# A two-block transformer kernel: in the second block the norm's scale moves from the activations to the finished tiles, its shift into ScalarE's functions, and the pooling from GpSimd to VectorE

## What is computed

```
h = rms_norm(x, ln1_g[l]) * (1.0 + sc1) + sh1
z = h @ w_in[l]
u_pool, c_q_raw, c_kv_raw, k_rope_raw, gz_a, gz_b = jnp.split(z, cuts, axis=-1)
y_a = pool_mixer(u_pool, w_pool[l], pool_scale[l]) @ p_pool[l]
y_b = mla(c_q_raw, c_kv_raw, k_rope_raw, ...) @ p_attn[l]
merged = jax.nn.sigmoid(gz_a) * y_a + jax.nn.sigmoid(gz_b) * y_b
x = x + g1 * (merged @ w_out[l])
h2 = rms_norm(x, ln2_g[l]) * (1.0 + sc2) + sh2
x = x + g2 * (jnp.square(jax.nn.relu(h2 @ w_ff1[l])) @ w_ff2[l])
```

## Time and profile before

| | us |
|---|---|
| time, median of 3 runs | 1953.87 (1952.1 to 1955.76) |
| the profiled execution's own time | 1956.42 |
| its span in the trace | 1955.1 |
| TensorE busy with matmuls | 1899.5 (97%) |
| VectorE / ScalarE / GpSimd busy | 1374.3 / 1032.3 / 35.3 |
| second block, from the first leading pair | from about 1243 to the end |

### The profile page before, as it was taken

The page is one execution under the profiler, slowest core; times in us unless marked ns, Lnnn a source line. Parts: engine busy times, 40 slices in busy tenths (PEclk is TensorE's granted clock), DMA queues, the critical chain, the costliest instruction groups (busy, mean ns, idle before and its releaser), DMA issues.

```text
span 1955.1 us, 36640 instructions
## 1 busy us (share of the span) xinstructions
PE 1899.5 (97%) x15339; PEld 1839.7 (94%) x15339; DVE 1374.3 (70%) x2295; ACT 1032.3 (53%) x1728; POOL 35.3 (2%) x56
## 2 busy tenths in 40 slices
PE   7999999999999999999999999899999998999998
PEld 6999988899999999989889999889999998999998
DVE  5777666577776677666568777677897566788854
ACT  5444555565444544455666444566554456655433
POOL 0000000000000000000000000030000003000000
PEclk9999999999999999999999999999999999999999
DMA  6777322346775577533245777334555544454553
GB/s 248 259 269 263 133 94 104 109 152 231 262 291 204 194 259 283 213 130 108 88 151 199 285 271 269 125 124 152 179 177 188 191 147 152 148 182 161 195 188 114
DMA packets 51812, 366.07 MB, mean 187 GB/s; under 512 B 6620, under 2 KB 8060, under 8 KB 9792
## 3 DMA queue, kind: packets, MB, share of 16 engines
q1 hardware_dynamic: 51648, 363.72, 52.5%
HBM read 362.65 MB, written 1.05 MB: 186 GB/s over the span
## 4 chain that ended last, share of the span: by engine, by line
PE 81%; DVE 9%; ACT 5%; DMA 2%; issue 2%; SPq 0%; DVEq 0%; ACTq 0%
PE bank L435 24%; PE bank L436 23%; PE bank L437 23%; DVE w_lo L1507 3%; ACT w_hi L1023 2%; DMA raw_a<-in_weights 2%; PE bank L471 1%; DVE full L1549 1%; PE bank L467 1%; PE bank L468 1%; PE bank L700 1%; PE bank L750 1%; PE bank L752 1%; PE bank L751 1%; PE bank L573 1%
## 5 line engine op out<-in xcount | busy, mean ns | idle before, releaser
L435 PE MATMUL bank<-xn_hi,w_hi 128*128 128x256 f32 (+1 forms) x2480 | 716.9, 289 | 6.1 <-DVE w_lo L1507 6.1
L437 PE MATMUL bank<-xn_lo,w_hi 128*128 128x256 f32 (+1 forms) x2480 | 706.9, 285 | 0.0
L436 PE MATMUL bank<-xn_hi,w_lo 128*128 128x256 f32 (+1 forms) x2480 | 705.2, 284 | 0.0
L1507 DVE TENSOR_TENSOR w_lo<-raw_a,w_hi 128x1024 fp32r<-128x1024 f32 (+1 forms) x282 | 356.4, 1266 | 180.5 <-ACT w_hi L1023 179.9
L435 PEld LDWEIGHTS bank<-xn_hi,w_hi 128*128 128x128 f32 x2480 | 467.1, 188 | 15.6 <-issue 13.1
L1507 DVE TENSOR_TENSOR w_lo<-raw_b,w_hi 128x1024 fp32r<-128x1024 f32 (+1 forms) x282 | 356.5, 1266 | 176.5 <-ACT w_hi L1023 175.7
L436 PEld LDWEIGHTS bank<-xn_hi,w_lo 128*128 128x128 f32 x2480 | 466.5, 188 | 1.0
L437 PEld LDWEIGHTS bank<-xn_lo,w_hi 128*128 128x128 f32 x2480 | 467.3, 188 | 0.0
L1023 ACT ACTIVATE w_hi<-raw_a 128x1024 fp32r<-128x1024 f32 (+1 forms) x282 | 306.3, 1088 | 231.9 <-PE bank L437 187.5
L1023 ACT ACTIVATE w_hi<-raw_b 128x1024 fp32r<-128x1024 f32 (+1 forms) x282 | 306.5, 1088 | 225.2 <-PE bank L437 201.9
L437 PE MATMUL bank<-h_lo,w_hi 128*128 128x272 f32 (+1 forms) x704 | 201.5, 286 | 0.0
(11 more groups left out here) (320 smaller groups left out, 3003.4 us busy)
## 6 DMA issues: line engine op xcount, KB each, us to landing
raw_a<-in_weights SPq DMA_DIRECT2D x123, 1024.0 KB, 4.8
raw_b<-in_weights SPq DMA_DIRECT2D x123, 1024.0 KB, 4.8
ada_raw<-in_ada_w SPq DMA_DIRECT2D x48, 1024.0 KB, 4.9
raw_a<-in_weights SPq DMA_DIRECT2D x16, 1408.0 KB, 6.3
raw_b<-in_weights SPq DMA_DIRECT2D x16, 1408.0 KB, 5.9
c_rows<-in_c_rows SPq DMA_DIRECT2D x3, 512.0 KB, 3.6
raw_a<-in_weights SPq DMA_DIRECT2D x2, 768.0 KB, 4.6
raw_b<-in_weights SPq DMA_DIRECT2D x2, 768.0 KB, 4.1
```

Of the source, the lines that this page charges most:

```text
L435: pe.matmul(o, wh, xh, start=start, stop=False)
L436: pe.matmul(o, wl, xh, start=False, stop=False)
L437: return pe.matmul(o, wh, xl, start=False, stop=stop)
L1507: dve.tensor_tensor(lo, raw_of(c, u), hi.bitcast(F32), ALU.subtract).then_inc(*k.up("w_lo"))
```

## The change

All tiles of `mixer2` and `ff` that read the normed activations now read the ones with the gain alone, 258 columns wide, and `normalised` is gone from the second block. In its place `norm_scale` waits for `rstd` only. DVE moves every such tile out of PSUM itself (`scaled_tile`): it copies the shift column to SBUF and multiplies the tile by `rstd`. ACT then adds the shift as the bias of the function that it applies: Square and Identity for the latents, Identity for the rotary key and the pooling, Tanh for gates, Relu in `ff`. The squares for the latents' norms move from DVE to ACT, relu from DVE to ACT. The pooling goes from GpSimd's queue to a chain of DVE's (places 8 to 14), and ACT's part of it to a chain from place 9. In `attention2` DVE now ends a head's first step after the row maximum; reciprocal and probabilities are in the next place. `ff` uses four buffers in place of two and is written as a pipeline: scale tile n, square tile n-1, low part of tile n-2, split.

```diff
@@ leading_units (PE)
-        tiles_as_ready(u, 0, to if to == cols else slice(0, N + 2), c.xn_hi, c.xn_lo, ("g", *stage), norm)
-        tiles_as_ready(u + 2, 2, to, c.xn_hi, c.xn_lo, stage)
+        tiles_as_ready(u, 0, to, c.xn_hi, c.xn_lo, ("g", *stage), norm)
+        if to != TX:
+            tiles_as_ready(u + 2, 2, to, c.xn_hi, c.xn_lo, stage)
+        else:
+            for i in (2, 3):
+                tile(u + i, i, TX, c.xn_hi, c.xn_lo)
@@ mixer2 (PE)
-        chains = [(5, 12, latent("cq", c.sq2)), (6, 13, latent("ckv", c.sq)), (15, 34, attention2(l))]
+        chains = [(3, 12, latent("cq", c.sq2)), (5, 13, latent("ckv", c.sq)), (15, 34, attention2(l))]
...
+            if is_moved(at):
+                if at > 3:
+                    tile(u, b, TX, c.xn_hi, c.xn_lo, rows=64 if at == 5 else P)
+                free[b] = [("tile_v", ("n2", l, at))]
@@ mixer2 (ACT)
-        normalised(stage, TN, u0 + 2, bias=c.mod_all[:, l, 0:8])
+        norm_scale(stage, u0 + 2)
...
+            if is_moved(at):
+                act.wait_ge(*k.at("tile_v", ("n2", l, at)))
+                s = c.shift[:, at:at + 1]
+                if at < 5:
+                    name, kk, t = ("cq", at, c.cq) if at < 3 else ("ckv", at - 3, c.ckv)
+                    act.activation(squares[at], t[:, kk, :], ACT.Square, bias=s).then_inc(*k.up("square_a", (name, l, kk)))
+                    act.activation(t[:, kk, :], t[:, kk, :], ACT.Identity, bias=s).then_inc(*k.up("tile_a", (name, l, kk)))
...
+                    act.activation(c.gates2[:, j, :], c.gates2[:, j, :], ACT.Tanh, bias=s, scale=0.5).then_inc(*k.up("tile_a", ("gate", l, j)))
-                act.activation(c.gates2[:, j, :], bank[gate_bank(at)][:, TN], ACT.Tanh, scale=0.5).then_inc(*k.up("tile_a", ("gate", l, j)))
@@ ff (ACT)
+        for n in range(32):
+            split_hi(u + 4)
+            act.wait_ge(*k.at("tile_v", ("ff1", l, n)))
+            act.activation(f_of(c, n), f_of(c, n), ACT.Relu, bias=c.shift[:, n:n + 1]).then_inc(*k.up("tile_a", ("relu", l, n)))
+            if n:
+                high(n - 1)
+            u += 1
@@ new on DVE
+    def scaled_tile(u, dst, b, j, key, half=False, rows=P):
+        dve.wait_ge(k.sem["unit_done"], u + 1)
+        dve.tensor_scalar(c.shift[0:rows, j:j + 1], bank[b][0:rows, N:N + 1], 0.5 if half else 1.0, None, ALU.mult).then_inc(*k.up("tile_v"))
+        dve.tensor_tensor(dst, bank[b][0:rows, TN], c.rstd[0:rows, TB], ALU.mult).then_inc(*k.up("tile_v", key))
@@ attention2 (DVE)
                 dve.tensor_scalar(stat[:, 2:4], stat[:, 0:2], -scale, None, ALU.mult).then_inc(*k.up("att_v", ("max2", l, h)))
+            yield
+            if h < MH:
                 dve.wait_ge(*k.at("att_a", ("exp2", l, h, 1)))
@@ mixer2 (DVE)
+            if at < 5:
+                scaled_tile(u, c.cq[:, at, :] if at < 3 else c.ckv[:, at - 3, :], moved_bank(at), at, ("n2", l, at))
...
+            elif is_moved(at):
+                scaled_tile(u, c.gates2[:, gate_of(at), :], moved_bank(at), at, ("n2", l, at), half=True)
@@ ff (DVE)
+        for n in range(32):
+            if n > 3:
+                dve.wait_ge(*k.at("x_lo", ("f", l, n - 4)))
+            scaled_tile(u, f_of(c, n), gate_up_bank(n // 4, n % 4), n, ("ff1", l, n))
+            if n:
+                squared(n - 1)
+            if n > 1:
+                lowered(n - 2)
+            split_lo(u + 4)
+            u += 1
```

More of the change, by code:

```diff
@@ L940, in mixer2 @@
             finish(chains, at)
[L941 to L956, removed]
+            b = moved_bank(at)
+            if is_moved(at):
+                if at > 3:
+                    tile(u, b, TX, c.xn_hi, c.xn_lo, rows=64 if at == 5 else P)
+                free[b] = [("tile_v", ("n2", l, at))]
             elif at in (12, 13):
@@ L1066, in normalised, with norm_scale @@
                 act.wait_ge(k.sem["unit_done"], held)
[L1067 to L1070, removed]
+            act.activation(hi, f, ACT.Copy).then_inc(*k.up("x_hi", (*stage, kk)))
             if kk == 4:
                 split_hi(held + 2)
+    def norm_scale(stage, held):
+        split_hi(held)
+        split_hi(held + 1)
+        if stage == ("ln1", 0):
+            two_norms(stage)
+        else:
+            root_of_mean(7, TB, stage)
     def two_norms(stage):
@@ L1464, in ff, with high @@
         u, stage = FIRST["ff1", l], ("ff", l)
-        normalised(stage, TN, u + 2, bias=c.mod_all[:, l, 24:32])
-        for i in range(8):
-            for j in range(4):
-                split_hi(u + 4)
-                act.wait_ge(*k.at("tile_v", ("f", l, i, j)))
-                act.activation(c.f_hi[:, 4 * i + j, :], c.full[:, j % 2, 0:N], ACT.Copy).then_inc(*k.up("x_hi", ("f", l, i, j)))
-                u += 1
+        norm_scale(stage, u + 2)
+        def high(n):
+            act.wait_ge(*k.at("tile_v", ("f", l, n)))
+            act.activation(c.f_hi[:, n, :], f_of(c, n), ACT.Copy).then_inc(*k.up("x_hi", ("f", l, n)))
+        for n in range(32):
[5 more added lines that the diff above has]
+            u += 1
         for s in range(32):
@@ L1937, in mixer2 @@
         u0, stage = FIRST["mix2", l], ("ln1", l)
-        normalised(stage, TB, TN, c.gain[:, l, 0, :], u0 + 2, bias=c.mod_all[:, l, 0:8])
-        for j in range(2):
-            cq = c.cq[:, j, :]
-            dve.wait_ge(k.sem["unit_done"], u0 + j + 1)
-            dve.tensor_tensor(cq, bank[j][:, TN], c.rstd[:, TB], ALU.mult).then_inc(*k.up("tile_v"))
-            shifted(j, j)
-            dve.wait_ge(*k.newest("tile_v"))
-            dve.tensor_scalar(cq, cq, c.shift[:, j:j + 1], None, ALU.add).then_inc(*k.up("tile_v", ("cq0", l, j)))
-        chains = [(5, 12, latent(l, "cq", 3, c.sq2, c.cq, c.cq_hi, c.cq_lo, V_QG)),
-                  (6, 13, latent(l, "ckv", 2, c.sq, c.ckv, c.ckv_hi, c.ckv_lo, V_KVG)),
-                  (9, 13, k_rope(l)), (13, 18, q_rope(l)), (15, 34, attention2(l))]
+        norm_scale(stage, u0 + 2)
+        chains = [(3, 12, latent(l, "cq", 3, c.sq2[:, 0:N], [c.gate[:, 0, 0:N], c.gate[:, 1, 0:N]], c.cq, c.cq_hi, c.cq_lo, V_QG)),
+                  (5, 13, latent(l, "ckv", 2, c.sq[:, 0:N], [c.full[:, 0, 0:N]], c.ckv, c.ckv_hi, c.ckv_lo, V_KVG)),
+                  (6, 13, k_rope(l)), (8, 15, pooled(l)), (13, 18, q_rope(l)), (15, 34, attention2(l))]
         u = u0
@@ L2001, in ff, with squared, lowered @@
         u, stage = FIRST["ff1", l], ("ff", l)
[L2002 to L2019 removed]
+        norm_scale(stage, u + 2)
+        def squared(n):
+            dve.wait_ge(*k.at("tile_a", ("relu", l, n)))
+            dve.tensor_tensor(f_of(c, n), f_of(c, n), f_of(c, n), ALU.mult).then_inc(*k.up("tile_v", ("f", l, n)))
+        def lowered(n):
+            low(c.f_lo[:, n, :], f_of(c, n), c.f_hi[:, n, :], ("f", l, n))
+        for n in range(32):
[8 more added lines that the diff above has]
+            u += 1
+        squared(31)
+        lowered(30)
         for s in range(32):
```

200 lines of the change are left out of this document (87 added, 113 removed).

## The result

The changed kernel takes 1988.7 us (median of 4 runs, 1987.48 to 1989.85) against 1954.07 before: 34.6 us more, ratio 1.0177 with a 95% interval of 1.016 to 1.0195. The forecast was 1978.5 within 1957 to 1990. The profiled execution took 1989.85, 33.4 more than that of before.

The account below looks back on a forecast made before the run. PE bounds the kernel before; after the change DVE and ACT, waiting for each other in turn, bind mixer2. 1956.4 + 31.3 (mixer2) - 6.6 (ff) = 1981.1 us, as a median 1978.5; range 1957 to 1990.

Parts of the forecast that it names:

- upper bound: End of the range, 1990 us: passes at 0.51 and a shift at 0.15 move the layers by +6 each.
- The circle: mixer2 places with a normed tile: DVE and ACT wait in turn, 3.2 or 3.6 us against PE's 2.85.
- The walk: mixer2 summed by place from the leading pair's end to place 31: +15.8 us in layer 0, +15.5 in layer 1.
- PE is the bound again: Behind mixer2's place 31 no tile is scaled, so PE binds as before and none of the loss is made good.
- `ff`: Heads of ff gain 4.3 us a layer, wider matmuls cost 1.0: -3.3 a layer, -6.6 in all.
- The rest costs nothing: Pooling off GpSimd, SP's loads and DVE's wait for rstd at a layer's start add no time.
- the circle doesn't bind: Faster rival: mixer2 heads need no more than 7.0 us and PE's waits go; median 1928.5 us, chance 0.13.
- it binds only to place 17: Rival in mixer2: later heads go at PE's 7.04 us, layers lose 5.8 and 3.6; median 1956.7, chance 0.13.
- The first rival: The rival that the circle doesn't bind: 22.9 us of waits and 5.3 of gaps go, wider tiles cost 2.9; chance 0.13.
- The clock: Rival: PE at half clock behind five long waits a layer adds 17 us; median 1995.5, chance 0.09.
- the main one: The case that the circle binds through mixer2's heads, with ff's gain: median 1978.5 us, chance 0.65.
- PE that works slowly in front of a circle that binds loses nothing: Argument against the clock rival: half-clock matmuls in mixer2 cost no time where DVE and ACT bind.

Follow-up runs that it names:

- run 1: The changed kernel with one line added: in mixer2 ScalarE writes the next weights' high part ahead of its bias pass; 1949.27 us, ratio 0.9974.
- run 11: The changed kernel with throw-away matmuls ahead of PE's long waits for probabilities (places 17, 23, 25, 27, and 31 of layer 0); 1984.1 us, ratio 1.0146.
- run 4: The kernel before with only the shift buffer widened to 32 columns, so the second block's buffers lie 64 bytes higher; 1958.39 us, ratio 1.0019.
- run 2: The kernel before with only ff changed; mixer2, GpSimd's pooling and all addresses as before; 1947.81 us, ratio 0.9966.
- run 5: The changed kernel with the pooling back on GpSimd, its high and low parts at place 20; 1987.01 us, ratio 1.016.
- run 7: The changed kernel with each head's reciprocal and probabilities in the same place as its maximum, as before; 1980.64 us, ratio 1.0126.

## Why the prediction was right

The sign, the mechanism and its place were right, the size 8.7 us short (33.4 against 24.7 between the profiled executions). That the time still lies in the range, 1.3 us under its upper bound, is in part luck: the bound was worked out for longer passes and copies, and the missing time came from other things. By its own steps:

- **The circle** is shown, by run 1. Its price of a place was well read: place 20, from shift to shift, took 3.42 us (1705.12 to 1708.54) where 3.45 was forecast; place 19 took 5.53 (1699.59 to 1705.12) for 4.99, and 0.49 of that is the wait for PE's late score, which is gone in run 11 (4.94).
- **The walk**: place 17 was forecast at 70.0 and came at 71.9 and 71.1; place 31 at 131.5 and 129.1, and came at 134.5 and 131.6. Terms mis-sized by 5.6 us in both layers together. Of this, 3.0 stand ahead of place 17, and I can't assign them. The other 2.6 stand between places 17 and 31: the layers took 62.7 and 60.5 us there, 9.0 and 8.6 a head where about 8.2 stood. In run 11 they took 60.7 and 58.7, so the clock is 3.8 us of it, more than the whole 2.6; without it the walk would have been 1.2 too long there.
- **"PE is the bound again" behind place 31** held, but not "as before": 46.1 and 44.6 us for 43.3. That is 4.1 us that the sum did not have. Layer 1 ran there at full clock; run 4 shows 6.4 ns more from start to start on each of the 192 matmuls over `y` by the address, 1.2 us of its 1.3. In layer 0 the half clock behind place 31 comes on top; run 11 takes 1.5 us of it away.
- **`ff`**: the heads took 8.6 for 12.86 us, as forecast. The leading pair ahead of them also became shorter, 6.21 us (1429.62 to 1435.83) for 7.26 (1408.25 to 1415.51), for which the sum had no term. With it a first product came from 96.84 to 92.41 us, and from 96.67 to 92.41 in layer 1: 8.7 less, where -6.6 stood. Alone, in run 2, `ff` is worth 6.5, with 4.3 to 9.2 as bounds. The second products, which the sum left as they were, took 0.7 us more each (90.45 to 91.13 in layer 0, and the same 91.13 in run 4): the address again.
- **"The rest costs nothing"** held for the pooling (run 5). The delay of probabilities by a place had no term of its own; the walk had it inside place 17's 5.7 us (5.4 and 5.9 measured), and run 7 prices it at 8.1 for all heads.
- **The rivals**: that the circle doesn't bind is refuted by run 1; that it binds only to place 17, by the 62.7 and 60.5 us from there to place 31, where this rival had 49.3. (The first rival's 2.9 us for wider tiles should be 3.6 by its own 1.4 ns, and the bounds count 27 moves and 33 passes a layer where the queues have 26 and 32; nothing hangs on either.) The clock was no separate case, as I had it, but a part of the main one. "PE that works slowly in front of a circle that binds loses nothing" was the step that failed: run 11 wins 4.6 us there. How much of the rival's 17 us was paid in all stays open, as run 11 left the waits for the latents' sums as they were. The Trainium skill, "TensorE: Matmul & The Clock Gate", section "HAM oscillation — how this bites in real kernels", has every long gap followed by half clock. The windows under run 11 agree for places 17 and 31: 0.50 and 0.57 behind the gaps, 1.00 where they are filled.

## What to carry to other kernels

Before work on one engine is made to depend on another, write down for one tile the ring that the waits and both queues form; its length, not the busy shares, must stay under the time of a tile on the engine that bounds. Here VectorE was busy 68% and ScalarE 53%, and the cure was to issue what doesn't depend on the other engine (the weight split) ahead of what waits. A result that another engine needs early, such as the first head's probabilities, may deserve an exception from an order that is good for all the rest.

## What the runs showed of the hardware

I had not expected that 64 bytes of SBUF address change how far apart matmuls start: over `y`, 113.5 ns from start to start became 119.9, and the duration in the trace 276 became 283, with all else the same (run 4). In the whole it was 4.1 us, with 2 to 5.5 as bounds of the interval. Which offsets are good, and whether the moving operand or another buffer matters, was not tried.
